# The down product of a SwiGLU layer by seven block products for eight, in six passes over the contraction

## The reference

```python
h += W_out(concat[RMSNorm(attention), RMSNorm(short gated conv)])
n = rms_norm(h, g_ffn)
h = h + (silu(n @ w_gate) * (n @ w_up)) @ w_down         # 2048 -> 5632 -> 2048
gate = sigmoid(rms_norm(h, g_ple) @ w_ple_gate)
h = h + gate * (p @ w_ple_proj)
```

## Time and profile before

| | |
|---|---|
| median of 3 runs | 2503.22 us (2502.7 to 2503.6) |
| the profiled execution | 2504.16 us, of which the span of instructions is 2502.6 us |
| PE busy | 2471.1 us, 99% of the span, 20366 matmuls |
| DVE, ACT, POOL busy | 1708.1 us (68%), 968.0 us (39%), 219.1 us (9%) |
| granted TensorE clock | 0.995 |
| moved by DMA | 324.02 MB |

### The profile page before, as it was taken

The page is one execution under the profiler, slowest core; times in us unless marked ns, Lnnn a source line. Parts: engine busy times, 40 slices in busy tenths (PEclk is TensorE's granted clock), DMA queues, the critical chain, the costliest instruction groups (busy, mean ns, idle before and its releaser), DMA issues.

```text
span 2502.6 us, 51598 instructions
## 1 busy us (share of the span) xinstructions
PE 2471.1 (99%) x20366; PEld 2456.1 (98%) x20366; DVE 1708.1 (68%) x2077; ACT 968.0 (39%) x1311; POOL 219.1 (9%) x237
## 2 busy tenths in 40 slices
PE   7999999999999999999999999999999999999998
PEld 7999999999999989999999999999999999999998
DVE  6777787778786888888888888888433323356433
ACT  5343334333433454444444444444322212233331
POOL 1120111011100000000000000000000000143000
PEclk9999999999999999999999999999999999999999
DMA  6353333333343424343343434343665443233332
GB/s 210 120 161 101 117 109 127 113 113 106 122 144 98 156 98 140 120 142 123 130 141 119 135 118 142 126 135 118 214 223 170 161 146 113 81 90 107 111 113 68
DMA packets 99887, 324.02 MB, mean 129 GB/s; under 512 B 18275, under 2 KB 18787, under 8 KB 99313
## 3 DMA queue, kind: packets, MB, share of 16 engines
q1 hardware_dynamic: 72288, 250.25, 30.6%
q0 software_dynamic: 26672, 70.69, 8.2%
q10 hardware_dynamic: 864, 2.24, 0.2%
HBM read 286.80 MB, written 40.65 MB: 131 GB/s over the span
## 4 chain that ended last, share of the span: by engine, by line
PE 83%; DVE 10%; issue 3%; DMA 2%; ACT 1%; DVEq 0%; SPq 0%; ACTq 0%
PE acc L591 15%; PE acc L595 15%; PE acc L593 15%; PE acc L795 7%; PE acc L796 7%; PE acc L794 7%; PE aux L795 5%; PE aux L794 5%; PE aux L796 5%; DVE tmp L1562 2%; DVE wlo L1330 1%; DMA wraw<-in_w_down 1%; DVE tmp L1335 1%; DVE q_both L1447 1%; ACT whi L962 1%
## 5 line engine op out<-in xcount | busy, mean ns | idle before, releaser
L1330 DVE TENSOR_TENSOR wlo<-wraw,whi 128x1024 fp32r<-128x1024 f32 (+1 forms) x276 | 333.6, 1209 | 364.3 <-ACT whi L962 363.6
L962 ACT ACTIVATE whi<-wraw 128x1024 fp32r<-128x1024 f32 (+1 forms) x276 | 285.7, 1035 | 667.6 <-PE acc L595 593.2
L591 PE MATMUL acc<-slots_a,whi 128*128 128x260 f32 x1536 | 312.8, 285 | 0.0
L595 PE MATMUL acc<-slots_a,wlo 128*128 128x260 f32 x1536 | 309.0, 282 | 0.0
L593 PE MATMUL acc<-slots_a,whi 128*128 128x260 f32 x1536 | 308.9, 283 | 0.0
L1679 DVE TENSOR_TENSOR wlo<-wraw,whi 128x1024 fp32r<-128x1024 f32 x176 | 215.2, 1223 | 104.4 <-ACT whi L1137 104.4
L591 PE MATMUL acc<-slots_b,whi 128*128 128x260 f32 x1312 | 264.3, 283 | 0.0
L593 PE MATMUL acc<-slots_b,whi 128*128 128x260 f32 x1312 | 264.0, 283 | 0.0
L595 PE MATMUL acc<-slots_b,wlo 128*128 128x260 f32 x1312 | 264.0, 282 | 0.0
L1137 ACT ACTIVATE whi<-wraw 128x1024 fp32r<-128x1024 f32 x176 | 186.2, 1058 | 155.3 <-DVE wraw L1672 83.9
L591 PEld LDWEIGHTS acc<-slots_a,whi 128*128 128x128 f32 x1536 | 238.0, 189 | 1.1 <-issue 0.5
(11 more groups left out here) (314 smaller groups left out, 5908.7 us busy)
## 6 DMA issues: line engine op xcount, KB each, us to landing
wraw<-in_w_in SPq DMA_DIRECT2D x96, 512.0 KB, 3.5
blocks<-in_w_gate SPq DMA_DIRECT2D x88, 512.0 KB, 4.1
blocks<-in_w_up SPq DMA_DIRECT2D x88, 512.0 KB, 3.7
wraw<-in_w_down SPq DMA_DIRECT2D x48, 448.0 KB, 3.5
wraw<-in_w_out SPq DMA_DIRECT2D x32, 512.0 KB, 3.5
wraw<-in_w_ple_gate SPq DMA_DIRECT2D x32, 512.0 KB, 3.5
slots_b<-f_dram SPq DMA_DIRECT2D x28, 520.0 KB, 4.6
f_dram<-sig_t POOLq DMA_DIRECT2D x22, 520.0 KB, 3.2
```

Of the source, the lines that this page charges most:

```text
L591: mm(to[:, h, :], w_h, x[:, 0, h * HALF:(h + 1) * HALF], start=begin, stop=False)
L595: done = mm(to[:, h, :], w_l, x[:, 0, h * HALF:(h + 1) * HALF], start=False, stop=end)
L962: on(whi[:, u % HILO, 0:width], wraw[:, u % RAW, 0:width], ACT.Copy).then_inc(s_whi, 1)
L1330: V.tensor_tensor(wlo[:, u % HILO, 0:width], wraw[:, u % RAW, 0:width], whi[:, u % HILO, 0:width].bitcast(F32), ALU.subtract).then_inc(s_w ...
```

## The change

Down is made by seven block products for eight too. An output pair g % 8 of pass g // 8 is a "group"; GROUPS = 48. A pass takes 3 or 4 contraction pairs (PASS), so a unit has 9 or 12 matmuls, and there are D_UNITS = 336 of them in the order DOWN_UNITS, where kind 0 of the next group comes before kinds 4 and 6 of this one. The weights are stored by blocks on the host, as those of gate and up are. Per group SP loads four blocks of 128 x 384 or 128 x 512, DVE makes four sums and seven low parts, ACT seven high parts, and the rings now hold DEEP = 8 half-size units. The seven parts of the activations are made in the gate and up stage (`hidden_sums`, on DVE) and stored in 14 half-tiles per pair instead of 8; a pass loads its parts into the same buffers that gate and up used, during the pass before. The results go into `stage(g)` and are added to the residual `hid2_pair` by a transfer with `accum_op=ALU.add` that POOL starts. The squares of the last norm move from POOL to ACT and DVE, the copies of the ple projection from DVE to ACT, and the loops of this part are written out. The scratch for POOL's descriptors is set to 4096 bytes. The diff, cut to its core:

```diff
-DOWN = ((4,), (7, 7), (8, 7), (6, 5))
+PASS = (3, 4, 4, 4, 3, 4)
+GROUPS = KP2 * PASSES
+DEEP = 2 * HILO
...
+DOWN_UNITS = [(0, 0)] + [(g + (kind == 0), kind) for g in range(GROUPS) for kind in (1, 5, 2, 3, 0, 4, 6)
+                         if g + (kind == 0) < GROUPS]
...
 SP
+        for u, kind in enumerate(KIND_AT):
+            sp.wait_ge(s_unit, U_D - 7 + u + 1)
+            down_part(0, kind)
+        for g in range(1, GROUPS):
+            n = PAIRS + g
+            sp.wait_ge(s_sum, 4 * (n - 1) + 1)
+            down_block(g, down_11, 0, 0, l_11)
+            sp.wait_ge(s_wlo, DOWN_AT[g - 1, 2] + 1)
+            down_block(g, down_12, 0, 1, l_12)
+            sp.wait_ge(s_sum, 4 * (n - 1) + 4)
+            down_block(g, down_21, 1, 0, l_21)
...
+                down_part(c + 1, (0, 1, 5, 2, 3, 4, 6)[j - 1])
...
 PE
+        for g, kind in DOWN_UNITS:
+            pe.wait_ge(s_wlo, w + 1)
...
+            if kind == 1:
+                pe.wait_ge(s_q0, n + 1)
...
+            if kind == 6:
+                pe.wait_ge(s_1b, n + 1)
...
+            for p in range(PASS[c]):
+                mm(to, w_h, hi, start=begin and p == 0, stop=False, skip_group_check=not begin)
+                mm(to, w_h, lo, start=False, stop=False, skip_group_check=not begin)
+                done = mm(to, w_l, hi, start=False, stop=p == PASS[c] - 1, skip_group_check=not begin)
...
 ACT, per unit k of down: results of kinds 0, 1, 5, 6, then the high part of unit k + 8
+            if k + DEEP < D_UNITS:
+                down_hi_of(k + DEEP)
...
+            if q >= 1 and kind == 4:
+                ple_square(q - 1)
+                if q < KP2 - 1:
+                    for m in (2 * q - 2, 2 * q - 1):
+                        ple_hi(m)
...
 DVE, per unit k of down
+            if kind == 2:
+                dve.wait_ge(s_q0, n + 1)
+                if g >= 2:
+                    dve.wait_ge(d_acc[g % 2], 16 * (g // 2))
...
+                V.tensor_tensor(stage(g)[:, 0, 0:HALF], to, q0_t, ALU.add).then_inc(s_11, 1)
...
+            if k + DEEP < D_UNITS:
+                down_ahead(k + DEEP)
...
+            if k == 0:
+                pair_scaled(PAIRS - 1, up_t[:, :, :])
+            if k == 1:
+                hidden_last(PAIRS // 2 - 1, tmp[:, 2:4, :])
+            if k == 2:
+                hidden_sums(PAIRS // 2 - 1, tmp[:, 2:4, :], (d_flo[0], 48 * (PAIRS // 4)))
+            if k == 3:
+                hidden_lo(PAIRS // 2 - 1, tmp[:, 2:4, :])
+            if k == 4:
+                hidden_sums_lo(PAIRS // 2 - 1)
...
+            if q >= 2 and kind == 6:
+                ple_added(q - 1)
...
 POOL
+        for s in range(2):
+            pool.wait_ge(d_flo[s], 48 * (PAIRS // 4))
+        pool.wait_ge(s_wlo, U_D)
+        pool.dma_start(hid_b[:, :, :], h_dram[:, 0:10, :]).then_inc(l_hid, 16)
+        pool.dma_start(hid_a[:, :, :], h_dram[:, 10:KT, :]).then_inc(l_hid, 16)
+        pool.dma_start(p_t[:, :, :], p_tiles).then_inc(l_p, 16)
+        pool.wait_ge(l_hid, 32)
+        for g in range(GROUPS):
...
+            pool.dma_start(hid2_pair(g % KP2), stage(g), accum_op=ALU.add).then_inc(d_acc[g % 2], 16)
```

560 lines of the change are left out of this document (330 added, 230 removed).

## The result

The changed kernel takes **2601.89 us** (median; 2596.57 to 2603.27), the kernel before 2503.2: ratio 1.039, interval 1.0372 to 1.0408. That is 98 us slower, where 2469 us was predicted and 2446 to 2500 given. The profiled execution is the fastest, 2596.57 us, with a span of 2595.0, so 92.4 us above the span of before.

The account below looks back on a forecast made before the run. PE's matmuls were taken to bound the kernel, with DVE pacing down's 3-wide groups. Terms -63.2 + 18 + 2 + 4 + 3 + 2 + 0.2 gave -34 us, so 2469 us, range 2446 to 2500 (0.8).

Parts of the forecast that it names:

- -63.2 for 528 matmuls: Down: 3696 matmuls in place of 4224, at 0.1197 us each, save 63.2 us, all on the path.
- Gate and up nothing: Gate and up: DVE's extra sums, about 2.9 us per two pairs, stay hidden by a lead of four units: no cost.
- rival E: Gate and up: DVE cannot hide its additions, +10 to +20 us there, 2485 us; chance 0.04.
- DVE's loop, 9.3 and 7.7 us: Down: DVE's work per group, 9.3 us 4-wide against PE's 10.05, 7.7 us 3-wide against 7.54.
- Late first blocks, +4 (0 to 10): Down's 3-wide groups: next group's first block queues behind parts, landing 4 to 4.5 us after its start: +4 us.
- rival B: Down: the queues fill, accumulates moving their bytes twice, 8.2 us per 3-wide group; 2485 us (2480 to 2496), chance 0.17.
- Hand-over +18 (8 to 28): From gate and up into down: waits for group 1's block, hidden stores, residual and first accumulate cost 18 us.
- Clock +2: Hand-over: after two long waits PE's matmuls run a while at the 1.2 GHz level: +2 us counted.
- rival D: Down's DVE-bound 3-wide groups: gaps drop PE's granted clock to 1.2 GHz, +77 us, 2546 us; chance 0.03.
- Accumulates landing in 4 to 6 us: Down: expected sign that accumulating transfers land in 4 to 6 us; 4.5 was taken for the first.
- C: Down: the accumulate itself is the bound, at 100 GB/s in the engines: +45 us, 2515 us (2500 to 2560), chance 0.11.
- Gaps in the 4-wide passes (B or C): Down: PE gaps in the 4-wide passes would show the forecast wrong and point to rival B or C.

Follow-up runs that it names:

- tiny accumulates: Changed kernel with each accumulating transfer moving 8 columns in place of 1040: 2514.8 us; the same edit on both blocks doubled: 2464.0 us.
- both blocks doubled: Changed kernel with second buffers for down's first and third blocks, long part rows, hand-over reordered and skew stores spread: 2470.7 us, ratio 0.9864.
- the doubled buffer: Changed kernel with a second buffer for down's first block, asked for a whole group earlier: 2534.8 us, ratio 1.0130.
- one-line kernel: Kernel before with only the scratch for POOL's descriptors set to 4096 bytes: 2521.6 us, ratio 1.0080.

## Why the prediction was wrong

By its own steps; the sum was made against the profiled span, so the miss is 92.4 + 34 = 126 us.

- **-63.2 for 528 matmuls**: right. The count is 19842, and where PE has no gap it keeps its rate (837 in 100 us, 0.1195 each).
- **Gate and up nothing**: right (870.77 of 875 busy, no new wait; rival E is out).
- **DVE's loop, 9.3 and 7.7 us**: right as far as the trace can tell. With the crowd gone a 4-wide group takes PE's 10.02 to 10.05, and the 3-wide ones come 7.9 apart where nothing is late (7.86 to 7.99 with tiny accumulates and both blocks doubled, 8.10 in the mean with the pass's first one of 9.49), 7.7 having been forecast. Last pass forecast +3, measured 71.4 for seven groups against 7 x 10.05 = 70.4: +1.
- **Late first blocks, +4 (0 to 10), in the 3-wide groups alone: this is the step that failed.** The passes two to five took 381.0 us, against 305 by the forecast's terms (24 x 10.05, 8 x 7.7, and 2 of the 4): 76 more than forecast, and most of it in the 4-wide passes, where the term was nothing. I priced 1.06 MB of parts at 350 GB/s, 3 us, and a landing of 4 to 4.5; I left out the fourth block ahead of them, the accumulate beside them, which I had priced in rival B, and above all I asked only whether the block would be late against four units of PE, 5.7 us at 4-wide, and found those passes safe. It landed in 8.2 (the median of the 4-wide passes; 9.6 in the group shown). And I took lateness as a delay to be paid once, where it is a term of a loop: block, three units of DVE, first sum, next block; 9.6 + 0.7 + 3.0 = 13.3 us in the group shown and 12.0 in the mean of the 4-wide passes, where PE needs 10.05. What shows it is the doubled buffer: the median landing only went from 8.2 to 7.6, and the mean of the groups fell to 10.34.
- **Hand-over +18 (8 to 28)**: each event was named in its order, each size too small. In us after T, forecast and measured: group 1's block 5.6 and 10.0; PE's second unit 7.0 and some 12; kind 3's result T + 15 and 22.5; the last hidden stores landed 25 and 33; the residual loaded 34 and 49; the accumulate 39 and 56.6; PE's unit 21 at T + 41 and 59. That is +36, with the same two long waits. The price of a transfer that stands nearly alone had been used (4.2, 4.5, 9 us) where seven kinds of parts fill the queue. Then the loop begins, and T to g8 is 106 where the forecast's terms give 72 (8 x 7.7, and 18, less the eight units of 0.9 that DVE is ahead): 34 us of the miss. It can be mended in part (79.9).
- **Clock +2**: the level fell as said, on the gaps: 0.80 and 0.83 granted from 1779 to 1900, in the mended kernel (both blocks doubled) 0.87 in the first 66 us and 1.00 from 1840 on. It is in the 34 above and was not separated. Over the whole kernel the granted clock is 0.979, below the 0.98 that was to speak for rival D. But D's mechanism is not there: in the mended kernel's 3-wide pass, which DVE paces, the clock is 1.00 (2105 to 2160), and in the changed kernel's fourth pass it is 1.00 with 6.5 us of 100 idle. The low stretches are those with the most idle time: besides the first 100 us, 0.94 from 2191 to 2285, with 71.4 of 94 us busy.
- **Ple +0.2**: right within 2 us (216.1 us after down, 217.7 before).
- **Accumulates landing in 4 to 6 us**: 4.5 to 5.0 in the last pass once the parts have landed, and 5.5 to 10.2 in the second to fifth.
- **The mixers: no step at all.** The scratch was described ahead of the prediction and never priced there. 19 us, shown by the one-line kernel.

Together 76 + 34 + 19 less 2 in the last pass are 127. Of the rivals, B had the right price of an accumulate and the right queue, but took the sum of the bytes (8.2 us a group) for the limit; its 2485 was far off, because the bytes were not what held the changed kernel back: its DMA share was 0.75, and the mended one keeps PE full at 0.90. That the mended 3-wide pass comes near B's 8.2 (8.32) is not B's doing, for almost without the accumulates' bytes it still takes 8.10. D (2546) and C (2515, to 2560) came nearest in time and had the wrong mechanism: for D see the clock above, and for C DVE waited for an accumulate's own semaphore once in the hand-over, not in the passes. "Gaps in the 4-wide passes (B or C)" was the sign to look for, and it appeared with a third cause.

What stays open: how much of the first 80 us of down the clock takes, whether the DMA engines are what bounds them (in the mended kernel their share is 1.04 there, at 335 GB/s, and tiny accumulates give only 3.5 us), and why the small scratch lets POOL go on only every 15 us (this is near the 15.6 us in which a skew store lands; that it waits for that landing was not tried).

## What to carry to other kernels

Where a buffer is freed late in one round and needed early in the next, add up the loop (landing, the engines between, the freeing instruction), and compare that with the round, not the landing with the slack; the landing to use is one behind all that stands ahead of it in its queue and beside it in the others. If the loop is near the round, a second buffer for that one tile can do what less traffic does: here two spare buffers of 2 KB a partition gave 67 and 27 us, while removing traffic gave 78 (most parts) and 87 us (the accumulates). With both buffers and the other edits in, the accumulating transfers cost 7 us. And every line of a change has a stage in which it acts: a smaller scratch for POOL's descriptors is paid where POOL issues its largest strided stores, a thousand us before the edited stage.

## What the runs showed of the hardware

- An accumulating transfer within SBUF takes the engines 1.96 times a copy of the same bytes (196 against 385 GB/s at their share), and lands in 5.0 us even for 4 KB (tiny accumulates), in 4.5 to 5.0 for 520 KB in the last pass once the parts have landed, in 5.5 to 10.2 in the changed kernel's passes with parts.
- The DMA share alone does not tell whether PE starves: 0.75 with 208 GB/s and PE starved, 0.90 with 253 GB/s and PE full.
- The rows of 1040 bytes, feared beforehand by the analogy to rows of 512, cost no time against 3120 and 4160 (2534.8 and 2536.0 us; q1 at 304 and 312 GB/s).
- An issue on ScalarE's queue of a 512 KB store with a shifted source occupied ACT for up to 13.0 us (8.9 to 13.0 in four of seven); on POOL an issue took 1.1, with up to 15 us between issues with the small scratch.
